# Second expert product of a mixture-of-experts kernel: from one fp32 product to three fp32r products of split operands

## The reference, cut to what matters

```
def expert_block(args):
    tok, e = args
    xb = xpad[tok]                                  # 128 x 1024
    h = jax.nn.silu(xb @ w1[e]) * (xb @ w3[e])      # 128 x 256
    return h @ w2[e]                                # 128 x 1024
```

## Time and profile before

| | us |
|---|---|
| median of 3 runs | 2929.09 |
| lowest and highest | 2926.44, 2933.21 |
| span of the profiled execution | 2922.5 |
| TensorE, VectorE, ScalarE busy in the span | 2607.3, 1659.2, 1308.7 |

### The profile page before, as it was taken

One profiled execution on the slowest core, in us unless ns is written; L12 is line 12 of the kernel. 1 busy time (PEld: TensorE's weight loads), 2 busy tenths in 40 slices (PEclk: granted clock), 3 DMA queues, 4 the chain that ended last, 5 costly groups with the idle time before them and its releaser, 6 DMA issues. The chain is left out here.

```text
span 2922.5 us, 50877 instructions
## 1 busy us (share of the span) xinstructions
PE 2607.3 (89%) x11129; PEld 1616.5 (55%) x11130; DVE 1659.2 (57%) x3062; ACT 1308.7 (45%) x2097; POOL 510.7 (17%) x662
## 2 busy tenths in 40 slices
PE   7998999968999999999949998988799999999980
PEld 3434545446666666666614446744566666666650
DVE  3335643555656665665548308925566766765646
ACT  3115642145555554555513205621456655654641
POOL 0000000122222222222200000000222322222222
PEclk9998999989999999999979998999899999999995
DMA  6772012078978977877776201012789878887767
GB/s 257 292 280 61 1 64 74 34 282 304 343 266 306 348 276 254 299 273 254 257 291 245 94 0 61 1 55 81 280 300 330 325 292 309 323 307 257 294 220 295
DMA packets 143559, 649.00 MB, mean 222 GB/s; under 512 B 33936, under 2 KB 41104, under 8 KB 85500
## 3 DMA queue, kind: packets, MB, share of 16 engines
q1 hardware_dynamic: 80412, 423.94, 39.0%
q10 hardware_dynamic: 19552, 137.45, 13.1%
q0 software_dynamic: 43520, 86.68, 8.1%
HBM read 627.94 MB, written 91.31 MB: 246 GB/s over the span
## 5 line engine op out<-in xcount | busy, mean ns | idle before, releaser
L1953 PE MATMUL e_psH<-e_w13h,e_xh 128*128 x1184 | 594.5, 502 | 65.1 <-issue 37.4
L2136 DVE TENSOR_TENSOR e_w13l<-ring,e_w13h x512 | 592.5, 1219 | 81.2 <-ACT e_w13h L2041 78.3
L1979 PE MATMUL e_psY<-ring,e_gt 128*128 x1184 | 566.5, 606 | 5.1 <-ACT e_gt L2054 5.1
L2041 ACT CAST e_w13h<-ring x512 | 497.8, 1043 | 136.6 <-DMA ring<-in_exp_w 81.1
L1953 PE MATMUL e_psH<-e_w13l,e_xh 128*128 x1184 | 474.9, 401 | 0.0
L2149 DVE TENSOR_TENSOR e_xl<-e_psT,e_xh 128x512 fp32r<-128x512 f32 x296 | 196.6, 688 | 402.2 <-issue 201.1
L1939 PE MATMUL e_psT<-ident,e_xg 128*128 128x128 f32 x1184 | 324.6, 277 | 10.1 <-DMA e_xg<-h_rows,e_gidx 6.2
L1953 PEld LDWEIGHTS e_psH<-e_w13h,e_xh 128*128 128x128 f32 x1184 | 228.7, 193 | 181.6 <-issue 145.5
L1959 PE MATMUL e_psH<-e_w13h,e_xl 128*128 x1184 | 307.9, 402 | 0.0
L1979 PEld LDWEIGHTS e_psY<-ring,e_gt 128*128 128x128 f32 x1184 | 213.9, 190 | 163.5 <-issue 151.1
L2061 ACT CAST e_xh<-e_psT 128x512 fp32r<-128x512 f32 x296 | 169.7, 588 | 257.9 <-PE e_psT L1939 134.3
(11 more groups left out here) (297 smaller groups left out, 2875.8 us busy)
## 6 DMA issues: line engine op xcount, KB each, us to landing
ring<-in_exp_w SPq DMA_DIRECT2D x256, 1024.0 KB
ring<-in_exp_w ACTq DMA_DIRECT2D x130, 1024.0 KB
p_lead<-in_ada_w SPq DMA_DIRECT2D x44, 1024.0 KB, 6.4
v<-y_rows SPq DMA_DIRECT2D x54, 512.0 KB, 5.5
f_Y<-y_rows SPq DMA_DIRECT2D x12, 1536.0 KB, 12.7
ring<-in_c_w_in SPq DMA_DIRECT2D x6, 2048.0 KB, 12.4
ring<-in_sh_w SPq DMA_DIRECT2D x6, 1024.0 KB
h_rows<-r_hrow SPq DMA_DIRECT2D x10, 512.0 KB, 2.6
```

Source lines behind the costliest of these rows:

```text
L1953: nc.tensor.matmul(psH[par][:], xh[par][:, k * P:(k + 1) * P], w[:, bass.DynSlice(half, 1), :, k, :], start=(k == 0 and i == 0), stop=False)
L1979: mm = nc.tensor.matmul(psY[:, c * 512:(c + 1) * 512], gt[par][:, k * P:(k + 1) * P], raw2[:, bass.DynSlice(half, 1), k, c * 512:(c + 1) * ...
L2041: nc.scalar.copy(w13h[:, bass.DynSlice(half, 1), :, k, :].rearrange("p o u k n -> p (o u) (k n)"), raw13[:, bass.DynSlice(half, 1), :, k, ...
L2136: nc.vector.tensor_tensor(low, raw, high.bitcast(F32), ALU.subtract).then_inc(w13_lo, 1)
```

## The change

The second product is now made like the first. `gt` becomes a high and a low part, `gth` (ScalarE) and `gtl` (VectorE, a new `gate`), and w2 becomes `w2h` (ScalarE, a new `split2`) and `w2l` (VectorE, a new `rest2`). There is one pair of w2 buffers and the split is made for each block, also where two blocks share an expert. `down` issues twelve fp32r matmuls in place of four fp32 ones, and no longer waits for `w2_in` but for `w2_lo` and, ahead of the last four, `gt_lo`.

```
-            def down(b, par, code, between):
-                o, half = order_in(code), half_in(code)
-                pe.wait_ge(gt_ready, b + 1)
+            def down(b, par, between):
+                pe.wait_ge(gt_hi, b + 1)
                 wait_for(pe, y_ready, b)
-                pe.wait_ge(w2_in, 16 * o + 16)
+                for k in range(KF):
+                    pe.wait_ge(w2_lo, KF * b + k + 1)
+                    for i, w in enumerate((w2h, w2l)):
+                        for c in range(2):
+                            nc.tensor.matmul(psY[:, c * 512:(c + 1) * 512], gth[par][:, k * P:(k + 1) * P], w[:, k, c * 512:(c + 1) * 512],
+                                             start=(k == 0 and i == 0), stop=False)
+                    if k == 0:
+                        between()
+                pe.wait_ge(gt_lo, b + 1)
                 for k in range(KF):
                     for c in range(2):
-                        mm = nc.tensor.matmul(psY[:, c * 512:(c + 1) * 512], gt[par][:, k * P:(k + 1) * P],
-                                              raw2[:, bass.DynSlice(half, 1), k, c * 512:(c + 1) * 512], start=(k == 0), stop=(k == KF - 1))
-                    if k == 0:
-                        between()
+                        mm = nc.tensor.matmul(psY[:, c * 512:(c + 1) * 512], gtl[par][:, k * P:(k + 1) * P],
+                                              w2h[:, k, c * 512:(c + 1) * 512], start=False, stop=(k == KF - 1))
                 mm.then_inc(y_mm, 1)
...
         @block.scalar
...
-                nc.scalar.copy(gt[par][:], psG[:, 0:F]).then_inc(gt_ready, 1)
+                nc.scalar.copy(gth[par][:], psG[:, 0:F]).then_inc(gt_hi, 1)
+
+            def split2(b, code):
+                act.wait_ge(w2_in, 16 * order_in(code) + 16)
+                act.sem_inc(act_clear, 1)
+                wait_for(act, y_mm, b)
+                for k in range(KF):
+                    nc.scalar.copy(w2h[:, k, :], raw2[:, bass.DynSlice(half_in(code), 1), k, :].rearrange("p o n -> p (o n)")).then_inc(w2_hi, 1)
...
                     rows_out(b - 1, m, 1 - par)
                     next2(b, code)
+                split2(b, code)
                 gate(b, par)
...
         @block.vector
...
+            def rest2(b, code):
+                for k in range(KF):
+                    dve.wait_ge(w2_hi, KF * b + k + 1)
+                    raw = raw2[:, bass.DynSlice(half_in(code), 1), k, :].rearrange("p o n -> p (o n)")
+                    nc.vector.tensor_tensor(w2l[:, k, :], raw, w2h[:, k, :].bitcast(F32), ALU.subtract).then_inc(w2_lo, 1)
+
+            def gate(b, par):
+                dve.wait_ge(gt_hi, b + 1)
+                nc.vector.tensor_tensor(gtl[par][:], psG[:, 0:F], gth[par][:].bitcast(F32), ALU.subtract).then_inc(gt_lo, 1)
...
                 rest13(b + 2, later)
                 indices(b + 4)
+                rest2(b, code)
+                gate(b, par)
```

More of the change, by code:

```diff
@@ L1816, in experts @@
         ge, g = sb("e_ge", [P, F]), sb("e_g", [P, F])
-        gt = [sb(f"e_gt{i}", [P, F]) for i in range(2)]
+        gth, gtl = ([sb(f"e_gt{n}{i}", [P, F], F32R) for i in range(2)] for n in "hl")
+        w2h, w2l = (sb(f"e_w2{n}", [P, KF, D], F32R) for n in "hl")
         ysb = [sb(f"e_y{i}", [P, D]) for i in range(2)]
@@ L1823, in experts @@
         (w13_in, w2_in, w13_hi, w13_lo, sel_ready, idx_mm, tok_ready, idx_ready, g_copied, s_copied, xg_clean, xt_mm, x_hi,
-         x_lo, h_mm, e_ready, g_ready, gt_mm, gt_ready, y_mm, y_ready, pool_clear, sp_clear, act_clear) = (sem(n) for n in (
+         x_lo, h_mm, e_ready, g_ready, gt_mm, gt_hi, gt_lo, y_mm, y_ready, pool_clear, sp_clear, act_clear, w2_hi, w2_lo) = (sem(n) for n in (
              "w13_in", "w2_in", "w13_hi", "w13_lo", "sel_ready", "idx_mm", "tok_ready", "idx_ready", "g_copied", "s_copied",
-             "xg_clean", "xt_mm", "x_hi", "x_lo", "h_mm", "e_ready", "g_ready", "gt_mm", "gt_ready", "y_mm", "y_ready",
-             "pool_clear", "sp_clear", "act_clear"))
+             "xg_clean", "xt_mm", "x_hi", "x_lo", "h_mm", "e_ready", "g_ready", "gt_mm", "gt_hi", "gt_lo", "y_mm", "y_ready",
+             "pool_clear", "sp_clear", "act_clear", "w2_hi", "w2_lo"))
         slots, slots_in = sb("slots", [P, P * (KMAX + 1)]), sem("slots_in")
@@ L1965, in turn_gate @@
                 pe.wait_ge(g_ready, b + 1)
-                wait_for(pe, gt_ready, b)
+                wait_for(pe, gt_lo, b)
                 for k in range(KF):
@@ L1995, in step @@
                 else:
-                    down(b - 1, 1 - par, before, lambda: index(b + 4, par, later))
+                    down(b - 1, 1 - par, lambda: index(b + 4, par, later))
             n = pairs(pe)
@@ L2003, in _ @@
                 turn(0, 0, 0, k)
-            step(0, 0, 0, None, code[0], code[4], True)
-            step(1, 1, 1, code[0], code[1], code[5])
+            step(0, 0, 0, code[0], code[4], True)
+            step(1, 1, 1, code[1], code[5])
             with pe.Fori(0, n - 1) as i:
-                code = codes(pe, 2 * i + 1, 7)
-                step(2 * i + 2, i + 1, 0, code[0], code[1], code[5])
-                step(2 * i + 3, i + 2, 1, code[1], code[2], code[6])
+                code = codes(pe, 2 * i + 2, 6)
+                step(2 * i + 2, i + 1, 0, code[0], code[4])
+                step(2 * i + 3, i + 2, 1, code[1], code[5])
             m = ending(pe)
-            code = codes(pe, m + 1, 2)
-            hidden(m + 2, 0, code[1], lambda k: turn_gate(m + 1) if k == 2 else None)
-            down(m + 1, 1, code[0], lambda: None)
+            code = codes(pe, m + 2, 1)
+            hidden(m + 2, 0, code[0], lambda k: turn_gate(m + 1) if k == 2 else None)
+            down(m + 1, 1, lambda: None)
             turn_gate(m + 2)
-            down(m + 2, 0, code[1], lambda: None)
+            down(m + 2, 0, lambda: None)
         @block.scalar
@@ L2099, in _ @@
             next2(m + 2, code[0])
+            split2(m + 2, code[0])
             gate(m + 2, 0)
@@ L2175, in _ @@
             m = ending(dve)
+            code = codes(dve, m + 2, 1)
             product(m + 2, 0)
+            rest2(m + 2, code[0])
+            gate(m + 2, 0)
 def combine(nc, s, a, l, tiles):
```

2 lines of the change are left out of this document (1 added, 1 removed).

## The result

The changed kernel takes 3007.59 us (median of 4 runs, 3001.18 to 3009.63), the kernel before on the same chip 2929.6 us: ratio 1.0275, 95% interval 1.0252 to 1.0298, 78 us slower. Forecast were 39. The profiled execution took 3001.18 us, its span is 2999.4 us.

The account below looks back on a forecast made before the run. VectorE was taken to set the changed kernel's pace: 45 pairs losing 1.0 us (0.6 pace, 0.4 clock), less 6, give +39 us; span 2961.5 plus 6.6 makes 2968 us. Range 2905 to 3078 us, own spread 2935 to 3000.

Parts of the forecast that it names:

- VectorE's added work: `rest2` and `gtl` on VectorE add 2.64 us to each block, also where the expert stays.
- The row's pace of 1.155 us: Start-to-start time of `rest13`'s subtractions, used to price `rest2` at 2.31 us a block.
- TensorE's saving: Twelve fp32r matmuls for eight fp32 records in the second product save 0.92 us a block, 1.16 at most.
- The read does not wait for the engine: VectorE's queue reads the table at its loop head while the engine still works on `rest2` and `gtl`.
- The first rival: VectorE's table read waits until the engine is empty, leaving the head bare: +149 us, 3078 us; chance 0.17.
- 1.4 us stay bare: VectorE's loop head: 4.0 + 0.2 us to issue against 2.8 us of covering work leave 1.4 us a pair.
- the sum's picture: VectorE's read starts behind `indices`, with `rest2` and `gtl` covering part of the head; 1.4 us bare a pair.
- The semaphores should not hold the queue back.: `w2h` is ready 3.5 to 4.5 us after `down(b-1)`, before VectorE reaches `rest2` after a 7.7 us step.
- 0.3 us each (-6 us): Some 20 pairs holding a block without `rest13` are led by TensorE and get 0.3 us faster.
- 3 us of slack: TensorE, with 19.3 us of work a pair, idles close to 3 us, most of it at its loop head.
- 1.0 us in 45 pairs: Pairs with two fresh experts that do not wait for transfers each get 1.0 us longer.
- the clock's part: Idle TensorE loses clock in one pair of two; after slack takes about half, this costs 0.4 us a pair.

Follow-up runs that it names:

- e7: The changed kernel without VectorE's two `rest2` subtractions, so the result lacks the low half of w2; 2899.13 us, ratio 0.9902.
- e15: The changed kernel without `rest2` (low half of w2 missing) and with TensorE's table read between the first and second product; 2883.72 us, ratio 0.9861.
- e2: The changed kernel with TensorE's table read moved between the first and second product, five registers instead of six; 2944.31 us, ratio 1.0064.
- e4: The changed kernel with 22 idle transposes at the end of each turn of TensorE's loop, to keep the clock up; 3111.79 us, ratio 1.0607.
- e17: The changed kernel with TensorE's read moved, VectorE's read split into four registers and two behind `rest13`, `choose` moved behind `rest13`; 2891.19 us, ratio 0.9906.
- e14: The changed kernel with one more VectorE operation a step, an unused sum over half of w2 ahead of `rest2`; 3096.45 us, ratio 1.0578.
- e16: The changed kernel with four steps instead of two in VectorE's loop body, nine registers a read, TensorE's head unmoved; 3008.16 us, ratio 1.0289.
- e18: The changed kernel with VectorE's read split into four and two registers and `choose` moved behind `rest13`, TensorE's head unmoved; 3033.91 us, ratio 1.0373.
- e3: The changed kernel with VectorE's table read moved behind the subtractions of `rest13`; 2996.65 us, ratio 1.0216.
- e12: The changed kernel with TensorE's read moved and the second of the two `rest2` subtractions made on GpSimd; 3063.5 us, ratio 1.0468.
- e6: The kernel before the change with TensorE's table read moved between the first and second product, seven registers; 2977.74 us, ratio 1.0195.

## Why the prediction was right in sign and wrong in size

- *VectorE's added work.* Right: a step of 10.60 us at the row above (10.34 forecast, and 10.52 in the mean of the new steps without a turn). The missing 0.2 is the gap ahead of `rest2`. The row's pace of 1.155 us was the right price of one behind another: the two of `rest2` take 2.36 us together, against 2.31 by that pace and 2.45 by 1.22 each. The busy time is 2031.9 us, 2080 were forecast, but with 2.9 us a block where the prediction's own sum has 2.64.
- *TensorE's saving.* Too large in the sum: from its first matmul to its last the second product takes 2.77 us, before 3.24 (medians, with `index` in between), and the last matmul is 0.22 us shorter, so 0.7 us a block and not 0.92 to 1.16. With `rest2` gone a new step is 10.79 us (e7) or, with TensorE's turn, 10.71 (e15), against 10.98: only 0.2 to 0.3 came through. VectorE idles 2 us a step in both, nearly all of it at the turns; what sets the pace there is open.
- *The read does not wait for the engine.* Right: it starts at 1108.0 while `rest2` runs until 1108.88. The first rival is out.
- *1.4 us stay bare.* Mis-sized: 1.00 a step, 2.0 a pair. The sum let the read start behind `indices`. In 50 of 71 turns it starts only when the last wait ahead of it is met, that for ScalarE's copy of the turned gate, and 2.37 us stay bare. In most of the other 21 the sum's picture holds, with 1.71.
- *"The semaphores should not hold the queue back."* This is the step that failed, in two ways. It looked at `w2_hi` alone, and with a step of 7.7 us. In a same step VectorE gets there 4.6 us earlier and waits 3.09 us for ScalarE, so the pairs with one did not gain 0.3 us each (-6 us) but lost 1.07 in the first layer and 0.01 in the second (+15 us). And it left out the turned gate, through which TensorE's head, the slower clock behind it and ScalarE's own head delay both `rows_in` and VectorE's read. In the sum TensorE had 3 us of slack at its turn; e2, with its head elsewhere, was 63 us faster, so the turn was not free, above all in the same steps.
- *1.0 us in 45 pairs.* A pair of new steps lost 0.95 and 0.93 us. That it agrees is luck in good part. The three pairs of the earlier trace rows on which both paces stand were short ones: in the mean such a pair took 22.40 and 21.89 us before, not 21.34 and 21.07, and 23.35 and 22.82 after, not 22.1 and 21.5, so that the error of some 1 us cancels. The forecast has 0.6 of pace and 0.4 of clock, and the clock's part was never measured by itself (e4, meant for it, moved the turn). The pairs were 50, not 45: those that waited for transfers were not spared. VectorE's idle time ahead of `e_w13l` was 81.2 us before and is 17.1 us after, so that slack has been spent.
- The remainder: 50 pairs x 0.94 = 47, 15 in the mixed ones, some 5 at the ends of the layers' runs of steps and 10 outside them make 77. Of the last 10 us 7 lie between the last block of the first layer and the first of the second, where nothing was changed; that stretch took 622 to 636 us in the runs, so they may be no effect of the change. Of the 38 us by which the loss was forecast too small, 21 are thus the pairs with a same step, 15 lie at the ends and outside the blocks, and 2 are the pairs of new steps.

So the change is slower because VectorE's 2.6 us a block go into a step in which VectorE, with its own loop head, had little room left; in the new steps 0.36 of the 0.51 us stay even with TensorE's head moved (e2), and go when VectorE's own head is shortened behind it (e17). TensorE's head, through the turned gate and ScalarE's copies, adds the rest, and 1.55 us to a same step. It isn't slower by necessity: with TensorE's read moved and VectorE's shortened (e17) a new step takes 10.98 us, the same as in the kernel before, a same step 8.32 against 10.13, and the three fp32r products pay.

## What to carry to other kernels

A loop head costs an engine only what is bare, but heads of several engines add up where the wait ahead of one engine's read depends on what stands behind another's. Look for the last wait ahead of each read, and ask which engine meets it. An idle time put down to "issue" may hide a second chain that ends at the same moment. Added work tells of it only if it does not cover the read as well: split the turns by what their read follows, as for e14, before you pay for removing the idle time (e16). A cure that loses 26 us alone (e18) can be worth 53 behind another one (e17). And take the pace from all pairs, not from three.

## What the runs showed of the hardware beyond the forecast

- The table read's load was longer the more registers it filled, with a wide spread. Medians on VectorE: 0.52 us for two (0.52 to 0.62), 1.63 for seven (1.03 to 3.00, changed kernel), 1.86 for eight (1.84 to 2.24, e3), 2.31 for nine (2.06 to 3.59, e16). With four, in e17 and e18, it took 0.35 to 2.91 us. Each register operation behind it takes 0.15 us on TensorE and ScalarE and 0.18 to 0.19 on VectorE:

```profile
L1841 DVEq FUSED_REGOPS  x9: 183/183/190, 1108.9 to 1111.1; - x9
...
L1841 DVEq TENSOR_LOAD <-table x1: 2094/2094/2094, 1106.8 to 1106.8; - x1
```

(e16). The Trainium skill's figure for the depth of VectorE's queue (Advanced Engine Details and Errata, Engine Queue Depths), cited in the prediction, was not put to a test: no run shows it holding the read back.

- A subtraction of 128x1024 fp32 took 2.45 us on GpSimd in the median (2.34 to 3.46) and 1.23 on VectorE (e12). The two did not run side by side: where VectorE's started second it ended 1.08 to 1.09 us behind GpSimd's (61 of them). GpSimd's was stretched to 2.96 to 3.46 us in 19 cases, and ended some 2.2 us behind the VectorE subtraction that had started ahead of it in 18 of these. `rows_in`, which reads one operand from PSUM, took its 0.68 us beside it.
- The same turn of TensorE's loop gained 63 us in one kernel and lost 55 in the other (e2, e6), whose TensorE programs differ in the second product and in the registers read, five and seven.
